# The openings of four feed-forward networks: when weight parts are made ahead of activations, and when side transfers begin

## The chip, the cores and the metric

One Trainium2 chip, one of its cores. The metric is the device time of one execution in microseconds (us). The kernel before takes 2700.04 us, the median of three runs (2699.19 to 2700.79).

A core has TensorE (PE, the matrix engine; its weight load is listed apart as PEld), VectorE (DVE), ScalarE (ACT), GpSimd (POOL) and SyncE (SP). Each takes its instructions in the order in which they are written; semaphores join them. Transfers between HBM and the on-chip memory run on 16 DMA engines. Here SP issues the loads of the weights and POOL issues the side transfers, in two DMA queues (q1 and q0).

## The reference

Two blocks of two layers each, all in float32, 256 tokens of width 1024. The change touches the first block's four plain networks, `swiglu`, numbered 0 to 3 here ("the first" to "the fourth"), and the loading of the second block's modulation weights, which are worked on beside them:

```python
def rms_norm(x, g, eps=NORM_EPS):
    x32 = x.astype(jnp.float32)
    y = x32 * lax.rsqrt(jnp.mean(x32 * x32, axis=-1, keepdims=True) + eps)
    return (y * g.astype(jnp.float32)).astype(x.dtype)

def swiglu(h, w_gate, w_up, w_down):
    return (jax.nn.silu(h @ w_gate) * (h @ w_up)) @ w_down

    for layer in range(DEPTH):
        x = x + 0.5 * swiglu(rms_norm(x, ffn_norm[layer, 0]), ffn_w_gate[layer, 0],
                             ffn_w_up[layer, 0], ffn_w_down[layer, 0])
        h = rms_norm(x, mix_norm[layer])
        ...                       # attention mixer (layer 0) or RWKV-7 time mixing (layer 1)
        x = x + 0.5 * swiglu(rms_norm(x, ffn_norm[layer, 1]), ffn_w_gate[layer, 1],
                             ffn_w_up[layer, 1], ffn_w_down[layer, 1])

def adaln(cond, w_mod, b_mod):    # second block: per layer, for two condition vectors
    m = jax.nn.silu(cond) @ w_mod + b_mod
    return [t[:, None, :] for t in jnp.split(m, N_MOD, axis=-1)]
```

So the order is: network 0, attention, network 1, network 2, RWKV-7, network 3, and then the second block with three more networks of another make, which the change leaves alone.

## The kernel before

**Weights.** All weights are packed in the order of use as tiles of 16 blocks of 128x128 floats, 1 MB each. SP loads them one after the other into a ring of three slots (`ring`); the load of tile T waits until TensorE has begun tile T-2 (semaphore `freed`). TensorE multiplies float32 as three products of rounded parts. Of each tile ScalarE copies the high part (`high(t)`, L1624, two halves) into one of two buffers `w_parts`, VectorE subtracts to get the low part (`low(t)`, L2158, two halves), and TensorE does three matmuls a block (L616, L617, L618). As there are two buffers, `high(t)` waits for the load of tile t and for TensorE having begun tile t-1.

**A network** has 33 tiles. Tiles come in threes: 16 blocks of gate, 16 of up, 16 of down weights, for 256 columns of the hidden width; `gate` and `up` write a PSUM bank each, the activation (silu of one times the other) is made by ScalarE and VectorE, and `down` adds into four banks. Numbered from 0: tile 0 is the first gate, 1 the first up, 2 and 3 are the second gate and up, 4 is the first down, 5 and 6 are the third gate and up, 7 is the second down, and so on.

**The opening.** The first gate and up tiles work on x times the gain (`h_parts`), before the root of the mean square is known. When VectorE has its reciprocal (L2294), the product of gate 0 is scaled (`scale_gate(0)`, L2260), ScalarE takes the silu in place (`scaled_silu(0)`, L1656) and VectorE finishes the activation (`scaled_activation(0)`, L2264, L2184, L2187 and one L2158). Tiles 2 and 3 are still done on `h_parts`, with `scale_gate(1)` and so on after them. From tile 5 on TensorE reads the normed input, `normed_parts`, which VectorE (eight instructions of L2302), ScalarE (`normed_high`, L1651) and VectorE again (`normed_low`) make in the opening. After tile 6 the order is that of a loop (L1686, L2315).

**The closing.** The last down tile ends bank by bank, and VectorE adds each of four banks to x (L2342, `x_ready`; after the mixers L2348). The next network's tile 0 is split before that: ScalarE's `high_first` stands ahead of `scaled_high` (which copies the four quarters of x as `h_parts`, L1645), and VectorE's `first_low(2, (0,))` stands ahead of the first add and `first_low(2, (1,))` ahead of the third. After RWKV-7 both halves of `first_low(3)` stand ahead of all four adds.

**Side transfers.** Beside each of the four networks a quarter of the second block's modulation runs: POOL loads two condition rows, spread over the partitions (0.5 MB each), and eight groups of modulation weights (1.5 MB each) into two buffers, `mod_w[0]` and `mod_w[1]`; VectorE works a group off in each half step of the loop (L2245) and counts `mod_used`, 8 to a network. Groups from the third on wait for their buffer. All of it stands in POOL's `ffn(n)`, L469 to L485. In the fourth network the context and the rope tables (1 MB and 0.6 MB) come first.

## Time and profile before

| | |
|---|---|
| median of three runs | 2700.04 us |
| the profiled execution: its time, its span | 2704.08 us, 2700.3 us |
| TensorE busy, weight load busy | 2652.0 us (98%), 2458.9 us (91%) |
| VectorE, ScalarE, POOL busy | 2121.3 us, 1292.1 us, 109.4 us |
| chain that ended last | PE 88%, DVE 5%, ACT 3%, DMA 3% |
| tile loads | 374 of 1024 KB, 4.8 us from issue to landing (median) |
| modulation weights, condition rows | 32 of 1536 KB, 8.2 us; 8 of 512 KB, 6.6 us |

Busy TensorE is nearly the whole span; what is not its own work is a few stalls, each found in the timeline as a matmul with idle time before it and the engine that ended it. A time in a timeline is counted from the span's start; merged rows have a count, and their length runs from the first's start to the last's end. The profile of one execution is 2704.08 us against a median of 2700.04 us, so differences are worked out inside the profile and then put on the median.

### The profile page before, as it was taken

The page shows a single profiled execution, that of the slowest core. Times are in us where ns is not written, and L with a number is a line of the kernel's source. Part 1 is how long each engine was busy: PE and PEld are TensorE (multiplying, and loading weights), DVE is VectorE, ACT ScalarE, POOL GpSimd, SP SyncE. Part 2 cuts the span into 40 slices and gives each one's busy share as a digit, 9 for nine tenths or more (in the row PEclk, how much of TensorE's full clock was granted, in tenths as well). Part 3 has the DMA queues.
Part 4 walks back from the last instruction along what each step waited for, and adds up shares of the span by engine and source line. Part 5 has one row for each costly group of instructions (what it writes and reads, how often), then busy time and mean ns, then how long its engine had stood idle before and what let it go on. Part 6 is the DMA issues. An engine that isn't in the chain of part 4 may idle for free.

```text
span 2700.3 us, 51095 instructions
## 1 busy us (share of the span) xinstructions
PE 2652.0 (98%) x20514; PEld 2458.9 (91%) x20514; DVE 2121.3 (79%) x3219; ACT 1292.1 (48%) x1780; POOL 109.4 (4%) x109
## 2 busy tenths in 40 slices
PE   8999999999999999999999999999999999999999
PEld 7998799999888989999879999986899999859999
DVE  7986589899765647995987878499878887987877
ACT  5345553443532324335565544555554464564543
POOL 0000000000013310000000000000000000000000
PEclk9999999999999999999999999999999999999999
DMA  7764267667431015764424455431345544404454
GB/s 273 280 233 157 94 258 279 238 253 280 155 140 63 1 73 219 280 233 172 157 79 156 166 185 183 168 141 63 110 156 187 188 156 155 153 19 145 168 186 155
DMA packets 61229, 456.22 MB, mean 169 GB/s; under 512 B 6840, under 2 KB 6864, under 8 KB 8736
## 3 DMA queue, kind: packets, MB, share of 16 engines
q1 hardware_dynamic: 54432, 395.86, 40.1%
q0 software_dynamic: 6656, 58.35, 5.4%
q8 instruction: 104, 1.70, 0.2%
q14 instruction: 37, 0.30, 0.0%
HBM read 453.12 MB, written 1.07 MB: 168 GB/s over the span
## 4 chain that ended last, share of the span: by engine, by line
PE 88%; DVE 5%; ACT 3%; DMA 3%; issue 1%; DVEq 0%; SPq 0%; ACTq 0%
PE ps L777 22%; PE ps L616 14%; PE ps L617 14%; PE ps L618 14%; PE ps L1058 3%; DMA ring<-in_weights 3%; PE ps L1452 3%; PE ps L1459 1%; ACT arena L2087 1%; PE ps L1311 1%; PE ps L1148 1%; PE ps L1141 1%; PE ps L558 1%; PE ps L1294 1%; DVE w_parts L2158 1%
## 5 line engine op out<-in xcount | busy, mean ns | idle before, releaser
L1624 ACT ACTIVATE w_parts<-ring 128x1024 fp32r<-128x1024 f32 x462 | 463.4, 1052 | 402.3 <-PE ps L616 284.9
L616 PE MATMUL ps<-normed_parts,w_parts 128*128 128x256 f32 x2160 | 602.3, 279 | 1.7 <-DVE w_parts L2158 1.7
L617 PE MATMUL ps<-normed_parts,w_parts 128*128 128x256 f32 x2160 | 603.7, 279 | 0.0
L618 PE MATMUL ps<-normed_parts,w_parts 128*128 128x256 f32 x2160 | 603.0, 279 | 0.0
L2158 DVE SCALAR_TENSOR_TENSOR w_parts<-ring,w_parts 128x1024 fp32r<-128x1024 f32 x462 | 544.6, 1220 | 50.0 <-ACT w_parts L1624 49.4
L777 PE MATMUL ps<-stream_high,half_parts 128*128 128x256 f32 x2224 | 422.8, 286 | 2.5 <-DVE half_parts L2363 1.6
L616 PEld LDWEIGHTS ps<-normed_parts,w_parts 128*128 128x128 f32 x2160 | 406.0, 188 | 2.3 <-DVE w_parts L2158 2.3
L618 PEld LDWEIGHTS ps<-normed_parts,w_parts 128*128 128x128 f32 x2160 | 406.0, 188 | 0.0
L617 PEld LDWEIGHTS ps<-normed_parts,w_parts 128*128 128x128 f32 x2160 | 405.9, 188 | 0.0
L2363 DVE SCALAR_TENSOR_TENSOR half_parts<-ring,half_parts 128x1024 fp32r<-128x1024 f32 x225 | 271.9, 1213 | 130.3 <-ACT half_parts L1711 129.4
L777 PEld LDWEIGHTS ps<-stream_high,half_parts 128*128 128x128 f32 x2224 | 347.9, 188 | 7.6 <-issue 5.6
L616 PE MATMUL ps<-act_parts,w_parts 128*128 128x256 f32 x1232 | 344.2, 279 | 1.9 <-DVE w_parts L2158 1.6
L617 PE MATMUL ps<-act_parts,w_parts 128*128 128x256 f32 x1232 | 344.3, 279 | 0.0
L618 PE MATMUL ps<-act_parts,w_parts 128*128 128x256 f32 x1232 | 344.0, 279 | 0.0
L1711 ACT ACTIVATE half_parts<-ring 128x1024 fp32r<-128x1024 f32 x225 | 235.9, 1059 | 204.9 <-PE ps L777 174.3
L777 PE MATMUL ps<-stream_low,half_parts 128*128 128x256 f32 x1112 | 310.4, 279 | 0.0
L616 PEld LDWEIGHTS ps<-act_parts,w_parts 128*128 128x128 f32 x1232 | 231.6, 188 | 3.5 <-DVE w_parts L2158 2.6
L2245 DVE CUSTOM_DVE_ANT_0 arena<-arena 128x1024 f32<-128x1024 f32 x192 | 227.2, 1221 | 7.6 <-DVE vec L2325 6.5
L618 PEld LDWEIGHTS ps<-act_parts,w_parts 128*128 128x128 f32 x1232 | 231.6, 188 | 0.0
L617 PEld LDWEIGHTS ps<-act_parts,w_parts 128*128 128x128 f32 x1232 | 231.5, 188 | 0.0
L777 PEld LDWEIGHTS ps<-stream_low,half_parts 128*128 128x128 f32 x1112 | 209.3, 188 | 3.3 <-issue 3.1
L2824 DVE SCALAR_TENSOR_TENSOR arena<-arena,vec 128x256 f32<-128x256 f32 x360 | 154.1, 480 | 2.3
(459 smaller groups left out, 4197.2 us busy)
## 6 DMA issues: line engine op xcount, KB each, us to landing
ring<-in_weights SPq DMA_DIRECT2D x374, 1024.0 KB, 4.8
arena<-in_mod_weights POOLq DMA_DIRECT2D x32, 1536.0 KB, 8.2
arena<-in_cond POOLq DMA_DIRECT2D x8, 512.0 KB, 6.6
arena<-toeplitz_rows POOLq DMA_DIRECT2D x1, 1536.0 KB, 12.3
x<-in_x SPq DMA_DIRECT2D x1, 1024.0 KB, 4.7
arena<-in_ctx POOLq DMA_DIRECT2D x1, 1024.0 KB, 5.4
out<-x SPq DMA_DIRECT2D x1, 1024.0 KB, 3.9
const<-in_const SPq DMA_DIRECT2D x1, 999.0 KB, 11.4
```

Source lines behind the costliest of these rows:

```text
L616: first = pe.matmul(into, wh, high, start=start, stop=False, skip_group_check=True)
L617: pe.matmul(into, wh, low, start=False, stop=False, skip_group_check=True)
L618: return first, pe.matmul(into, wl, high, start=False, stop=stop, skip_group_check=True)
L777: mm = pe.matmul(into, stationary, moving, start=start and n == 0, stop=stop and n == 2, skip_group_check=True)
L1058: mm = pe.matmul(ps[:, mm_n[0] % 4, m * S:(m + 1) * S], w.take(), mixed[i][:, k, :], start=(k == 0), stop=(k == KT - 1))
L1452: mm = pe.matmul(ps[:, two_banks(j) + tt, 0:keys], q[:, tt * P:(tt + 1) * P], k, start=True, stop=True)
L1624: a(w_parts[:, to, 0, cols], ring[:, at, cols], ACT.Copy).then_inc(s["w_high"], 1)
L1711: a(half_parts[:, u % 3, 0, :], ring[:, tile % RING, half * HALF:(half + 1) * HALF], ACT.Copy).then_inc(s["half_high"], 1)
L2158: return stt(out=out, in0=whole, scalar=1.0, in1=high, op0=ALU.mult, op1=ALU.subtract)
L2245: ins = nc.vector.tensor_tensor_reduce(into, mod_w[half][:, q, :], cond_row[c], 1.0, 0.0, ALU.mult, ALU.add, mod_part[:, at, c:c + 1])
L2363: stt(out=half_parts[:, u % 3, 1, :], in0=ring[:, (t["tile"] + tile) % RING, half * HALF:(half + 1) * HALF], scalar=1.0, in1=half_parts[:, ...
L2824: ins = stt(out=conv[:, b, :], in0=src, scalar=wt, in1=conv[:, b, :], op0=ALU.mult, op1=ALU.add)
```

## The change

Two edits. In the opening, ScalarE does `high(3)` ahead of `scaled_silu(0)`; VectorE does `low(3)` ahead of `scaled_activation(0)`, `low(4)` ahead of the eight instructions that norm the input, and `scale_gate(1)` after `normed_low`. On POOL's queue other waits stand ahead of the side transfers: the second group of network 0 waits for its second gate product; network 1's condition rows and first group wait for the last logits of the attention (`dl_max`) and its second group for the x after it; network 2's wait for the last modulation group of network 1; network 3's wait for nothing of their own.

```diff
@@ -475,11 +475,17 @@
-                if n:
-                    pool.wait_ge(s["x_ready"], (0, 2, 3, 5)[n] * QUARTERS)
+                if n == 1:
+                    pool.wait_ge(s["dl_max"], GROUP)
+                if n == 2:
+                    pool.wait_ge(s["mod_used"], 2 * MOD_ROUNDS)
                 for c in range(2):
                     pool.dma_start(cond_row[c], d["cond"][:, c * D:(c + 1) * D].broadcast_to((P, D))).then_inc(s["cond_in"], 16)
                 for g in range(MOD_ROUNDS):
+                    if n == 0 and g == 1:
+                        pool.wait_ge(s["gate_ready"], 2)
+                    if n == 1 and g == 1:
+                        pool.wait_ge(s["x_ready"], 2 * QUARTERS)
@@ -1673,8 +1679,8 @@
+                high(3)
                 scaled_silu(0)
-                high(3)
                 high(4)
                 normed_high()
                 scaled_silu(1)
@@ -2293,8 +2299,9 @@
                 scale_gate(0)
+                low(3)
                 scaled_activation(0)
-                low(3)
+                low(4)
                 if ahead:
                     dve.wait_ge(s["std_ready"], NORMS[ahead["i"]] + 1)
...
+                normed_low()
                 scale_gate(1)
-                low(4)
-                normed_low()
                 low(5)
                 scaled_activation(1)
                 low(6)
```

In the kernel after, POOL's and ScalarE's lines stand 6 lower in the file, VectorE's 6 or 7, and POOL's DMAs at L483 and L491.

VectorE in the opening of each network, from the scaling of gate 0 to the second activation; the pairs of L2158 rows on `ring` are `low(3)`, `low(4)`, `low(5)` in this order. Before:

```order
L2260 TENSOR_TENSOR arena<-ps,rstd 128x512 [waits gate_ready,dve_step]
L2264 TENSOR_TENSOR arena<-arena,rstd 128x512 [waits gate_used]
L2184 TENSOR_TENSOR arena<-ps,arena 128x512 [waits up_ready,dve_step]
L2187 CAST act_parts<-arena 128x512 [waits dve_step]
L2158 SCALAR_TENSOR_TENSOR act_parts<-arena,act_parts 128x512 [waits dve_step]
L2158 SCALAR_TENSOR_TENSOR w_parts<-ring,w_parts 128x1024 [waits w_high] x2
L2302 SCALAR_TENSOR_TENSOR h<-x,vec,rstd 128x256 x8
L2260 TENSOR_TENSOR arena<-ps,rstd 128x512 [waits gate_ready]
L2158 SCALAR_TENSOR_TENSOR w_parts<-ring,w_parts 128x1024 [waits w_high] x2
L2158 SCALAR_TENSOR_TENSOR normed_parts<-h,normed_parts 128x512 [waits normed_high] x4
L2158 SCALAR_TENSOR_TENSOR w_parts<-ring,w_parts 128x1024 [waits w_high] x2
L2264 TENSOR_TENSOR arena<-arena,rstd 128x512 [waits gate_used]
```

The same place in the kernel after:

```order
L2266 TENSOR_TENSOR arena<-ps,rstd 128x512 [waits gate_ready,dve_step]
L2164 SCALAR_TENSOR_TENSOR w_parts<-ring,w_parts 128x1024 [waits w_high] x2
L2270 TENSOR_TENSOR arena<-arena,rstd 128x512 [waits gate_used]
L2190 TENSOR_TENSOR arena<-ps,arena 128x512 [waits up_ready,dve_step]
L2193 CAST act_parts<-arena 128x512 [waits dve_step]
L2164 SCALAR_TENSOR_TENSOR act_parts<-arena,act_parts 128x512 [waits dve_step]
L2164 SCALAR_TENSOR_TENSOR w_parts<-ring,w_parts 128x1024 [waits w_high] x2
L2309 SCALAR_TENSOR_TENSOR h<-x,vec,rstd 128x256 x8
L2164 SCALAR_TENSOR_TENSOR normed_parts<-h,normed_parts 128x512 [waits normed_high] x4
L2266 TENSOR_TENSOR arena<-ps,rstd 128x512 [waits gate_ready]
L2164 SCALAR_TENSOR_TENSOR w_parts<-ring,w_parts 128x1024 [waits w_high] x2
L2270 TENSOR_TENSOR arena<-arena,rstd 128x512 [waits gate_used]
```

Tile 3's low part now stands ahead of the first activation, tile 4's ahead of the norming, and the scaling of gate 1 (the second row `arena<-ps,rstd`) directly ahead of tile 5's low part.

ScalarE in the same opening, from the root to tile 5; rows `w_parts<-ring` that wait are the first halves of `high(3)`, `high(4)`, `high(5)`. Before:

```order
L1592 ACTIVATE std<-ps 128x256 [waits ss_ready]
L1656 ACT_TABLE_LOAD
L1656 ACTIVATE arena<-arena 128x512 [waits gate_scaled]
L1624 ACTIVATE w_parts<-ring 128x1024 [waits freed,tile_loaded0]
L1624 ACTIVATE w_parts<-ring 128x1024
L1624 ACTIVATE w_parts<-ring 128x1024 [waits freed,tile_loaded1]
L1624 ACTIVATE w_parts<-ring 128x1024
L1651 ACTIVATE normed_parts<-h 128x512 [waits h_ready] x4
L1656 ACTIVATE arena<-arena 128x512 [waits gate_scaled]
L1624 ACTIVATE w_parts<-ring 128x1024 [waits freed,tile_loaded2]
```

The same place in the kernel after:

```order
L1598 ACTIVATE std<-ps 128x256 [waits ss_ready]
L1630 ACTIVATE w_parts<-ring 128x1024 [waits freed,tile_loaded0]
L1630 ACTIVATE w_parts<-ring 128x1024
L1662 ACT_TABLE_LOAD
L1662 ACTIVATE arena<-arena 128x512 [waits gate_scaled]
L1630 ACTIVATE w_parts<-ring 128x1024 [waits freed,tile_loaded1]
L1630 ACTIVATE w_parts<-ring 128x1024
L1657 ACTIVATE normed_parts<-h 128x512 [waits h_ready] x4
L1662 ACTIVATE arena<-arena 128x512 [waits gate_scaled]
L1630 ACTIVATE w_parts<-ring 128x1024 [waits freed,tile_loaded2]
```

Only tile 3's high part moved; the table load for silu now comes after it, and the second silu still stands ahead of tile 5's high part.

POOL's queue around the third and fourth networks; the first four rows are the third network's side transfers, the rest the fourth's (`in_ctx` is the context). Before:

```order
L481 DMA arena<-in_cond 128x1024 [waits x_ready]
L481 DMA arena<-in_cond 128x1024
L485 DMA arena<-in_mod_weights 128x3072 x2
L485 DMA arena<-in_mod_weights 128x3072 [waits mod_used] x6
...
L476 DMA arena<-in_ctx 128x2048 [waits y_ready]
L477 DMA arena<-in_rope 128x1280
L481 DMA arena<-in_cond 128x1024 [waits x_ready]
```

And in the kernel after:

```order
L483 DMA arena<-in_cond 128x1024 [waits mod_used]
L483 DMA arena<-in_cond 128x1024
L491 DMA arena<-in_mod_weights 128x3072 x2
L491 DMA arena<-in_mod_weights 128x3072 [waits mod_used] x6
...
L476 DMA arena<-in_ctx 128x2048 [waits y_ready]
L477 DMA arena<-in_rope 128x1280
L483 DMA arena<-in_cond 128x1024 x2
L491 DMA arena<-in_mod_weights 128x3072 x2
```

The third network's condition rows wait for a count that is reached inside the second network; the fourth's follow the rope tables with no wait between.

## Rows read from the trace of the kernel before

**Rows 1.** Timeline, TensorE: start, us, engine, line, operation, count, [idle before <-releaser].
```profile
33.11 0.36 PE L616 MATMUL ps<-h_parts,w_parts 128*128 128x256 f32 x1 [2.08 <-DVE w_parts L2158]
356.69 0.48 PE L616 MATMUL ps<-h_parts,w_parts 128*128 128x256 f32 x1 [1.92 <-DVE w_parts L2158]
548.53 0.36 PE L616 MATMUL ps<-h_parts,w_parts 128*128 128x256 f32 x1 [2.12 <-DVE w_parts L2158]
1049.20 0.36 PE L616 MATMUL ps<-h_parts,w_parts 128*128 128x256 f32 x1 [2.06 <-DVE w_parts L2158]
```

**Rows 2.** Busy time by stretch: us, PE, PEld, DVE, ACT, POOL, PEclk, DMA, GB/s.
```profile
350.00:355.00 5.00, 4.76 (x41) 4.57 (x40) 4.16 (x6) 3.30 (x4) 0.00 (x0) 1.00 1.01 428
355.00:360.00 5.00, 3.31 (x16) 3.34 (x17) 5.00 (x10) 2.07 (x3) 0.00 (x0) 0.68 0.58 206
```

**Rows 3.** Timeline, ScalarE, third network's opening, 540 to 558.
```profile
541.26 1.28 ACT L1656 ACT_TABLE_LOAD   x1
546.07 2.00 ACT L1624 ACTIVATE w_parts<-ring 128x1024 fp32r<-128x1024 f32 x2 [1.65 <-DMA ring<-in_weights]
554.37 0.62 ACT L1656 ACTIVATE arena<-arena 128x512 f32<-128x512 f32 x1
555.02 2.01 ACT L1624 ACTIVATE w_parts<-ring 128x1024 fp32r<-128x1024 f32 x2
```

**Rows 4.** Timeline, VectorE, openings of the second, third and fourth networks.
```profile
351.41 0.69 DVE L2260 TENSOR_TENSOR arena<-ps,rstd 128x512 f32<-128x512 f32 x1
...
543.06 0.69 DVE L2260 TENSOR_TENSOR arena<-ps,rstd 128x512 f32<-128x512 f32 x1
544.45 0.69 DVE L2264 TENSOR_TENSOR arena<-arena,rstd 128x512 f32<-128x512 f32 x1 [0.70 <-ACT arena L1656]
...
557.89 2.35 DVE L2158 SCALAR_TENSOR_TENSOR w_parts<-ring,w_parts 128x1024 fp32r<-128x1024 f32 x2
...
1042.91 0.69 DVE L2260 TENSOR_TENSOR arena<-ps,rstd 128x512 f32<-128x512 f32 x1
```

**Rows 5.** Timeline, TensorE, tile 5 begins in the same three openings.
```profile
369.61 0.28 PE L616 MATMUL ps<-normed_parts,w_parts 128*128 128x256 f32 x1
...
560.25 0.28 PE L616 MATMUL ps<-normed_parts,w_parts 128*128 128x256 f32 x1
...
1062.04 0.28 PE L616 MATMUL ps<-normed_parts,w_parts 128*128 128x256 f32 x1
```

**Rows 6.** DMA issues at 517.0, 534.6, 343.0 and 1034.5, in this order.
```profile
ring<-in_weights SPq DMA_DIRECT2D x1, 1024.0 KB, 4.7
ring<-in_weights SPq DMA_DIRECT2D x1, 1024.0 KB, 11.4
ring<-in_weights SPq DMA_DIRECT2D x1, 1024.0 KB, 10.2
ring<-in_weights SPq DMA_DIRECT2D x1, 1024.0 KB, 12.2
```

**Rows 7.** Timeline, GpSimd's queue, third and fourth networks.
```profile
529.08 1.05 POOL L481 DMA_DIRECT2D arena<-in_cond  x2 [50.22 <-DVE x L2342]
...
999.64 0.59 POOL L476 DMA_DIRECT2D arena<-in_ctx  x1 [0.94 <-DVE h L2646]
```

**Rows 8.** Timeline, VectorE and ScalarE, from the second network's end to the third's beginning.
```profile
511.52 0.17 DVE L2325 TENSOR_TENSOR vec<-vec,arena 128x12 f32 x1 [0.17 <-DVE arena L2245]
...
523.66 1.23 DVE L2158 SCALAR_TENSOR_TENSOR w_parts<-ring,w_parts 128x1024 fp32r<-128x1024 f32 x1 [2.65 <-ACT w_parts L1624]
...
528.10 0.69 DVE L2342 SCALAR_TENSOR_TENSOR x<-ps,x 128x512 f32<-128x512 f32 x1 [0.28 <-PE ps L618]
...
527.85 1.89 ACT L1645 ACTIVATE h_parts<-x,vec 128x256 fp32r<-128x256 f32 x4 [0.62 <-DVE x L2342]
```

**Rows 9.** Timeline, ScalarE, before the fourth network.
```profile
1019.51 2.01 ACT L1624 ACTIVATE w_parts<-ring 128x1024 fp32r<-128x1024 f32 x2 [22.31 <-DMA ring<-in_weights]
...
1028.68 0.91 ACT L1645 ACTIVATE h_parts<-x,vec 128x256 fp32r<-128x256 f32 x2 [0.82 <-DVE x L2348]
```

## Prediction, written before the kernel after was run

> **What bounds the kernel now.** TensorE is busy nearly throughout, so I first listed its idle times in its timeline and kept those in the plain networks. Each opening has one of 2 us, at the first matmul of tile 3, which waits for VectorE's low part [rows 1]; together 2.08 + 1.92 + 2.12 + 2.06 = 8.2 us. Next came the busy time by stretch, because from tile 3 to tile 5 the second opening takes 369.61 - 356.69 = 12.9 us and the third only 560.25 - 548.53 = 11.7 [rows 1, 5]. In the stretch behind the second's stall the granted clock is 0.68, and 16 matmuls take 3.31 us, 0.207 us each, against 4.76 / 41 = 0.116 at full clock [rows 2]. So the engine ran some 3.3 us at 1.2 of 2.4 GHz after standing still for 1.9 us; that costs 16 x 0.091 = 1.5 us. The fourth opening (1062.04 - 1049.20 = 12.8) has such a spell too, the third has none, and I take none for the first, whose stall is like the third's. What the openings lose is thus 8.2 + 2 x 1.5 = 11.2 us at most.
>
> Why tile 3 is late is seen on ScalarE and VectorE: tile 3's high part begins at 546.07, after 1.65 us of waiting for its load [rows 3], and VectorE's low part stands behind the first activation, which itself waits 0.70 us for silu [rows 4]. The load took 11.4 us from its issue, and 10.2 and 12.2 in the second and fourth openings, where one issued before the side transfers takes 4.7 [rows 6]; POOL has issued its 4 MB 5.5 us before [rows 7]. The DMA engines are then full, at 428 GB/s [rows 2].
>
> **The openings.** The stall at tile 3 goes, in all four. With the side transfers issued earlier, tile 3's load is there in time (in the first network only its first group is ahead, 1.5 MB less, 3.7 us at 428 GB/s). In the third opening ScalarE starts tile 3's high part at 541.3, is done with it at 543.3, loads the table in 1.28 us [rows 3] and has the silu by 545.3; VectorE meanwhile makes the low part from 543.75 to 546.0. TensorE needs it at 546.4 and has it.
>
> What is late next is tile 5. ScalarE works in order: the second silu waits for `scale_gate(1)`, and that now stands behind `normed_low`, so tile 5's high part can't begin sooner. VectorE's work between the scaling of gate 0 and tile 5's low part is the same instructions as before in another order: 557.89 - 544.45 = 13.4 us without idle time [rows 4]. From the scaling's end, 543.06 + 0.69, that gives 557.2; then silu 0.62 and half of tile 5's high part, 2.01 / 2 [rows 3], with 0.1 for the hand-overs: 558.9; then half of the low part, 2.35 / 2 [rows 4]: 560.1. Before, tile 5 began at 560.25 [rows 5]. So the third opening gains 0.15 us: the stall moves from tile 3 to tile 5, where it is 2.1 + 0.15 less, about 1.9 us. The first opening is like it, 0.15. In the second the same 17.0 us from the scaling's start give 351.41 + 17.0 = 368.4 against 369.61, 1.2 us; in the fourth 1042.91 + 17.0 = 1059.9 against 1062.04, 2.1 us [rows 4, 5]. Sum 3.6 us, the two slow spells already gone in it. But four stalls of 1.5 to 2.2 us are there again, and before two of four such brought the slow clock: I put back two spells, 3.1 us. Openings: -3.6 + 3.1 = -0.5 us. Bounds: no spell -3.6, four spells +2.6.
>
> **The third network's side transfers.** They now wait for the count that VectorE completes at 511.4, just ahead of its sum at 511.52 [rows 8], 17.6 us sooner than at 529.08 [rows 7]. That falls into the closing of the second network. The tile load issued 5.5 us after the burst is then no longer tile 3 but tile 0 of the third network, issued at 517.0 [rows 6]. Issued so, three loads took 10.2, 11.4 and 12.2; I take the middle: it lands at 528.4 instead of 521.7. Queued behind it, in order: half its high part on ScalarE 1.05, half the low part on VectorE (1.23), two adds, the other half, two adds (0.6 each), and ScalarE's last quarter of h (0.9), 6.8 us with overlaps of pipeline ends [rows 8]. The last quarter is then ready at 535.2 instead of 527.85 + 1.89 = 529.74: 5.5 us late, and TensorE has little else to do. It stands idle for some 4 us in this, more than before the slow spells, so 1.5 us for one spell: +7.0 us. Bounds: landing after 10.2 us and no spell, +4.3; after 12.2 us and two spells, +9.4. What before hid in the opening (only tile 3) now meets the wait that TensorE can't be given other work for.
>
> **The fourth network's side transfers** wait for nothing of their own and follow the context at 999.64 [rows 7]. The queue then holds 1 + 0.6 + 1 + 3 MB, and SP's two tiles of the output projection come beside them: 8.0 million bytes, at 428 GB/s [rows 2] 18.7 us, until 1020. Tile 0's load is issued at 1014.7, into the last group's transfer. It landed at 1019.4, as ScalarE waited for it until 1019.51 [rows 9]; with half the burst gone I take 10.3 us, 1025.0. VectorE's and ScalarE's row of work behind it is as long as above, 6.8 us: 1031.8 against 1028.68 + 0.91 = 1029.6 [rows 9], +2.2 us. With a slow spell at even chance 0.8: +3.0. Bounds: nothing at all (it lands by 1022.8) and 12.2 us with two spells, 4.1 + 3.1 = +7.2. The projection's own last tile is issued one tile's work earlier and has the work of two to land: I count nothing for it.
>
> **The second network's** rows and first group start when the attention's softmax is nearly done, at a time without tile loads; its second group, alone, is issued when all four were before. Nothing is late by them: 0. **The first network's** second group waits for the second gate product, which ends where tile 3 begins (31 us, the stall's start in [rows 1]), and is first read in the loop; it shares the engines with tile 5's load, which is not wanted before the second silu, 10 us later: 0.
>
> **Sum.** -0.5 + 7.0 + 3.0 = +9.5 us within the profiled execution (2704.08 us, span 2700.3). The runs' median lies 4 us lower than it, with the same work, so I put the difference on the median: 2700.04 + 9.5 = 2709.5 us.
>
> A rule of the Trainium skill that speaks against the 11.4 us: DMA: Bandwidth & Descriptors, section "Queues, rings and completion order", says that each DMA engine goes round-robin between the queues that have work, packet by packet. By that, a tile beside the side transfers would get about half the engines and take some 7 to 9 us. The 10.2 to 12.2 of [rows 6] don't agree with it for a load issued just behind the condition rows.
>
> **Rivals.**
> - *The queues share evenly (same).* The shares would be by packets of 8 and 12 KB, 40% for the tile: its 1.05 MB at 0.4 x 428 GB/s take 6.1 us instead of 2.5, so 4.7 + 3.6 = 8.3 us. Tile 0 lands at 525.3, +2.4 us in the third network, and 1023.0, +0.2, in the fourth. Openings -0.5: +2.1, 2702.1 us. For it: only part of a burst is the rows, the slow beginning. Against: three of three loads so issued took longer.
> - *Tile 0's load goes first, the closings are untouched (faster).* Then only openings remain, -3.6 without spells: 2696.4 us. Against it the same three rows.
> - *Tile 5 is not late.* Then the openings give all of 11.2 us and the closings take 10: -1.2, 2698.8 us. It would need ScalarE to do tile 5's high part ahead of the second silu, which the order denies.
> - *All new gaps slow the clock (slower still).* Two more spells in the openings, one more in each closing: +9.5 + 3.1 + 1.5 + 0.8 = +14.9, 2714.9 us. The gaps in the closings are the longest.
>
> **How the numbers follow.** Forecast 2709.5 us with 0.60; even sharing 0.15; closings untouched 0.09; tile 5 not late 0.04; all spells 0.12. A measurement of this kernel tells 0.2%, 5.4 us, from no change. Slower by over that: nearly all of the first case, all of the last: 0.71. Faster by over that asks for untouched closings and a gain of the openings beyond 3.6 us, or both the second and third rival at once: 0.06. Same: 0.23. The range leaves out the untouched closings and half of the third rival at its lower end and little at its upper: 2700 to 2716 us.
>
> **What the profile after would show.** Right: no idle time at tile 3 and one of 1.5 to 2.2 us at tile 5 in each opening, released by VectorE; a tile load issued near 516 that takes over 10 us; ScalarE waiting for DMA ahead of the third network's tile 0 for some 6 us; the adds to x there 5 us later. Wrong: the tile load near 516 under 7 us, or TensorE reaching the third network's tile 1 no later than 534 less what the first two openings gain. If the closings cost nothing the whole forecast falls to the openings' half microsecond.

## The result and the profile after

The kernel after takes 2717.71 us (median of 9 runs, 2714.52 to 2719.61), against 2700.79 us for the kernel before in runs beside it. The ratio is 1.0056, 95% interval 1.0043 to 1.0069, so the change costs 11.6 to 18.6 us. The profiled execution took 2714.52 us with a span of 2712.6, against 2704.08 and 2700.3. The two spans differ by 12.3 us, and that is what the traces account for. The ratio and the medians give 15 to 17 us. The two profiled executions lie on opposite sides of their medians (before 3.3 us over, after 3.2 us under), and the other executions left no trace, so these 3 to 5 us stay unexplained.

The stalls of the plain networks are in TensorE's timeline of the kernel after, with the columns of [rows 1]. The L668 rows are the first matmuls of a network, the L622 rows tile 5:

```profile
45.92 0.35 PE L622 MATMUL ps<-normed_parts,w_parts 128*128 128x256 f32 x1 [3.15 <-DVE w_parts L2164]
...
371.95 0.55 PE L622 MATMUL ps<-normed_parts,w_parts 128*128 128x256 f32 x1 [2.38 <-DVE w_parts L2164]
...
535.00 0.47 PE L668 MATMUL ps<-h_parts,w_parts 128*128 128x256 f32 x2 [3.99 <-ACT h_parts L1651]
...
537.25 0.79 PE L668 MATMUL ps<-h_parts,w_parts 128*128 128x256 f32 x2 [0.74 <-ACT h_parts L1651]
...
570.53 0.35 PE L622 MATMUL ps<-normed_parts,w_parts 128*128 128x256 f32 x1 [2.39 <-DVE w_parts L2164]
...
1040.86 0.47 PE L668 MATMUL ps<-h_parts,w_parts 128*128 128x256 f32 x2 [1.86 <-ACT h_parts L1651]
...
1073.57 0.36 PE L622 MATMUL ps<-normed_parts,w_parts 128*128 128x256 f32 x1 [1.67 <-DVE w_parts L2164]
```

The four stalls of [rows 1] at tile 3 are gone. In each opening there is one at tile 5 in their place, 9.6 us together against 8.2, and two networks now begin with a stall that waits for ScalarE's parts of h. What delays these is seen on GpSimd's queue, ScalarE and VectorE; the rows to compare are [rows 7], [rows 8] and [rows 9]:

```profile
514.81 1.05 POOL L483 DMA_DIRECT2D arena<-in_cond  x2 [32.54 <-DVE arena L2251]
515.85 1.05 POOL L491 DMA_DIRECT2D arena<-in_mod_weights  x2
...
531.00 2.00 ACT L1630 ACTIVATE w_parts<-ring 128x1024 fp32r<-128x1024 f32 x2 [8.96 <-DMA ring<-in_weights]
532.09 1.23 DVE L2164 SCALAR_TENSOR_TENSOR w_parts<-ring,w_parts 128x1024 fp32r<-128x1024 f32 x1 [8.01 <-ACT w_parts L1630]
...
1035.73 1.06 ACT L1630 ACTIVATE w_parts<-ring 128x1024 fp32r<-128x1024 f32 x1 [27.45 <-DMA ring<-in_weights]
```

The burst (the condition rows and two groups of weights, 4 MB) begins at 514.81; in the kernel before it began at 529.08. Tile 0's load of the third network is issued at 520.11 and lands at 530.92, that of the fourth is issued at 1025.79. From issue to landing (last column, us) they take 10.8 and 9.8, where the kernel before took 4.7 for the third network's [rows 6]:

```profile
ring<-in_weights SPq DMA_DIRECT2D x1, 1024.0 KB, 10.8
...
ring<-in_weights SPq DMA_DIRECT2D x1, 1024.0 KB, 9.8
```

Busy time by stretch behind the third network's late start, columns as in [rows 2]:

```profile
530.00:535.00 5.00, 1.01 (x9) 0.84 (x8) 2.91 (x4) 3.05 (x5) 0.00 (x0) 1.00 0.80 338
535.00:540.00 5.00, 4.02 (x17) 3.53 (x18) 5.00 (x11) 4.37 (x11) 0.00 (x0) 0.54 0.62 210
540.00:545.00 5.00, 5.00 (x36) 5.00 (x36) 3.93 (x6) 1.96 (x3) 0.00 (x0) 0.78 0.01 3
```

TensorE does 1.01 us of work in 5, and in the next two stretches of 5 us its granted clock is 0.54 and 0.78 in the mean: it ran at 1.2 of 2.4 GHz from about 535.4 to 542.2, twice as long as the spell of [rows 2].

**Where the time went.** Both kernels, and those below, issue the same 20,514 matmuls in the same order, so each one's start can be set against its start before. By how much that difference grows in a part of the program is what the part costs; a closing is counted up to the next network's tile 1. The names of the other kernels are explained with their experiments. In us against the kernel before, one profiled execution each:

| | start, to 28 | 1st opening | 2nd opening | 3rd closing | 3rd opening | 4th closing | 4th opening | elsewhere | span |
|---|---|---|---|---|---|---|---|---|---|
| after | +0.5 | +2.4 | 0.0 | +7.4 | -0.2 | +2.5 | -1.5 | +1.2 | +12.3 |
| order only | -0.5 | +5.6 | +4.9 | +0.2 | +5.4 | 0.0 | +4.2 | +3.6 | +23.6 |
| waits only | -0.2 | -0.2 | +0.3 | +6.5 | +0.9 | +4.2 | -2.1 | -1.0 | +8.6 |
| late transfers | -0.1 | +3.1 | -1.0 | -0.1 | +5.2 | 0.0 | +3.1 | +0.3 | +10.6 |
| half burst | +0.8 | +0.6 | +1.0 | +4.5 | -0.2 | 0.0 | -1.5 | +2.0 | +7.1 |
| rows last | +0.7 | -0.1 | +0.5 | +6.4 | -0.2 | +2.0 | -1.6 | +1.7 | +9.4 |
| tile 5 ahead | -0.4 | +1.2 | -3.6 | +5.9 | -2.5 | +4.1 | -3.3 | -2.1 | -0.4 |
| spread | +0.7 | +0.4 | -0.9 | 0.0 | +1.4 | 0.0 | -1.6 | -2.5 | -2.3 |
| spread, tile 5 ahead | +0.4 | -2.3 | -2.5 | 0.0 | -2.4 | 0.0 | -3.3 | +3.6 | -6.6 |
| late, tile 5 ahead | +0.3 | -1.5 | -3.6 | -0.1 | +2.1 | 0.0 | 0.0 | -0.5 | -3.1 |
| spread, order as before | -0.6 | -0.2 | +1.5 | +0.6 | -0.2 | 0.0 | -2.1 | -2.2 | -3.1 |

The 3rd closing is the second network's end up to the third's tile 1, the 4th the output projection up to the fourth's tile 1; both are named by the network whose tile 0 may be late. The second opening's column holds that network's beginning too. By rounding and at the ends a row's sum differs from its span by up to 0.3. Each profiled execution lies somewhere in its kernel's spread (that of before 3 us over the median beside it, that of order only 5 over, that of spread 5 under). So the medians and their intervals below decide whether a kernel is faster, and the table tells only where the time goes.

### The profile page after: what moved, and what is told of

The parts are those of the page before. It is cut to its first block, busy times and chain, and to the rows that moved or that the text cites. A ratio compares the mean times of both kernels' runs of the same rounds, so it can differ in the third digit from the quotient of the medians.

```text
span 2712.6 us, 51095 instructions
## 1 busy us (share of the span) xinstructions
PE 2658.1 (98%) x20514; PEld 2464.3 (91%) x20514; DVE 2120.3 (78%) x3219; ACT 1291.5 (48%) x1780; POOL 109.5 (4%) x109
## 4 chain that ended last, share of the span: by engine, by line
PE 86%; DVE 7%; ACT 3%; DMA 2%; issue 1%; DVEq 0%; SPq 0%; ACTq 0%
PE ps L783 21%; PE ps L622 14%; PE ps L623 14%; PE ps L624 14%; PE ps L1064 3%; PE ps L1458 3%; DMA ring<-in_weights 2%; DVE w_parts L2164 1%; PE ps L1465 1%; ACT arena L2093 1%; PE ps L1317 1%; PE ps L1154 1%; PE ps L1147 1%; PE ps L564 1%; PE ps L557 1%
## 5 line engine op out<-in xcount | busy, mean ns | idle before, releaser
L622 PE MATMUL ps<-normed_parts,w_parts 128*128 128x256 f32 x2160 | 604.3, 280 | 11.3 <-DVE w_parts L2164 11.3
L622 PEld LDWEIGHTS ps<-normed_parts,w_parts 128*128 128x128 f32 x2160 | 407.4, 189 | 12.6 <-issue 10.3
L622 PE MATMUL ps<-act_parts,w_parts 128*128 128x256 f32 x1232 | 344.5, 280 | 1.3 <-DVE w_parts L2164 1.2
L622 PEld LDWEIGHTS ps<-act_parts,w_parts 128*128 128x128 f32 x1232 | 231.5, 188 | 2.7 <-DVE w_parts L2164 1.9
```

Source lines behind the costliest of these rows:

```text
L622: first = pe.matmul(into, wh, high, start=start, stop=False, skip_group_check=True)
```

## The experiments

Theory A is that of the forecast: early side transfers make tile 0's load late where TensorE has nothing else to do, and the new order moves the openings' stall from tile 3 to tile 5. Its rivals were that the loss comes from one of the two alone, that the order gains and the transfers cost, or that the two are one effect. The letters of the rivals begin anew in each expectation. The names are those of the table.

The runs of before beside each kernel gave 2702.41, 2701.72 and 2700.98 us (medians of 11, 33 and 19 runs). Line numbers in the rows differ by two to six between kernels.

**Order only**: the new order of the openings, the waits of before. That is the kernel after with GpSimd's side of the change undone; against the kernel after the edit is:

```
-                if n == 1: pool.wait_ge(s["dl_max"], GROUP)
-                if n == 2: pool.wait_ge(s["mod_used"], 2 * MOD_ROUNDS)
+                if n: pool.wait_ge(s["x_ready"], (0, 2, 3, 5)[n] * QUARTERS)
-                    if n == 0 and g == 1: pool.wait_ge(s["gate_ready"], 2)
-                    if n == 1 and g == 1: pool.wait_ge(s["x_ready"], 2 * QUARTERS)
```

> Only the new order of the openings; the side transfers start as in the kernel before. Theory A (the closings cost the time, the new order needs the early transfers): no cost in the closings; but tile 3's load is late again (10 to 12 us), and silu of gate 0 now stands behind tile 3's high part on ScalarE. Tile 5 begins 14.0 us after the first activation does, which begins some 4 us after tile 3's load lands: 48.6, 371.2, 564.0 and 1064.7 us against 44.8, 369.6, 560.3 and 1062.0, +11.9 us, and 0 to 6 us of slow clock behind stalls of some 5 us at tile 5. Total +12 to +18 us. Rival B (the order is worth its 2 us a stall by itself): -4 to -8 us. Rival C (the order is neutral, as worked out with early transfers): -0.5 us.

Measured: 2721.99 us, ratio 1.0071 (1.0058 to 1.0084), which is 16 to 23 us slower than before; theory A had 12 to 18. TensorE's stalls in the second and fourth openings:

```profile
361.46 0.36 PE L616 MATMUL ps<-h_parts,w_parts 128*128 128x256 f32 x1 [1.36 <-DVE w_parts L2158]
377.04 0.55 PE L616 MATMUL ps<-normed_parts,w_parts 128*128 128x256 f32 x1 [4.14 <-DVE w_parts L2158]
...
1066.39 0.36 PE L616 MATMUL ps<-h_parts,w_parts 128*128 128x256 f32 x1 [1.88 <-DVE w_parts L2158]
1081.97 0.36 PE L616 MATMUL ps<-normed_parts,w_parts 128*128 128x256 f32 x1 [4.14 <-DVE w_parts L2158]
```

The closings cost at most 0.2 us, and the openings cost 20 us. With late transfers tile 3's load is late as before, so its stall stays, and the one at tile 5 comes on top, at 2.60 to 4.14 us, where the expectation had some 5. The order alone is a loss. In the traces it is larger than that of the whole change (23.6 against 12.3 us); the intervals of the two ratios overlap.

**Waits only**: the new waits, the openings' order of before. Against the kernel before it is the edit above read the other way round.

> Only the new waits of the side transfers; the openings are in the old order. Theory A: the closings cost as in the changed kernel, 7.7 us before the third network and 3.2 before the fourth; tile 3's load is in time but its low part still stands behind the first activation, so the stall at tile 3 stays at 1.9 us in each opening (each 0.2 us shorter). Total +9 to +12 us. Rival B (the cost of the change is the slow clock behind the new gaps at tile 5): -1 to +1 us. Rival D (the queues share evenly): +2 us.

Measured: 2710.96 us, ratio 1.0037 (1.0023 to 1.0051), 10 us where theory A had 9 to 12.

```profile
32.93 0.36 PE L622 MATMUL ps<-h_parts,w_parts 128*128 128x256 f32 x1 [1.92 <-DVE w_parts L2164]
357.66 0.36 PE L622 MATMUL ps<-h_parts,w_parts 128*128 128x256 f32 x1 [1.92 <-DVE w_parts L2164]
530.70 1.50 PE L668 MATMUL ps<-h_parts,w_parts 128*128 128x256 f32 x4 [3.29 <-ACT h_parts L1651]
...
554.36 0.41 PE L622 MATMUL ps<-h_parts,w_parts 128*128 128x256 f32 x1 [1.92 <-DVE w_parts L2164]
```

The closings cost 6.5 and 4.2 us without any change of order. Tile 3's stall stays at 1.92 us in three openings, and is 1.05 us in the fourth, although its load is in time now: it had two causes, the load and VectorE's order, and either is enough.

**Late transfers**: the kernel after, the third and fourth networks' wait put back.

```
-                if n == 2: pool.wait_ge(s["mod_used"], 2 * MOD_ROUNDS)
+                if n >= 2: pool.wait_ge(s["x_ready"], (0, 2, 3, 5)[n] * QUARTERS)
```

> The changed kernel with the waits of the third and fourth networks' side transfers put back (x ready). Theory A: TensorE has no gap above 0.5 us before these networks; but their tile 3 is late again with silu behind it, tile 5 begins 22.7 us after the reciprocal's start in the third and 23.6 in the fourth (18.8 with early transfers). First and second networks as in the changed kernel. Total +4 to +9 us, so less than the change by 6 to 12. Rival B (the cost is in all four openings alike): the whole +15 stays. Rival C (only the closings matter, the openings are even): -0.5 us.

Measured: 2712.77 us, ratio 1.0042 (1.0028 to 1.0057), which is 11.3 us (8 to 15) where theory A had 4 to 9. Both closings are at zero, as expected. The expectation also had tile 5 begin 3.9 and 4.8 us later in the two openings than with early transfers; against the kernel after they cost 5.4 and 4.6 us more, as much as the closings gain. The third's rows on ScalarE and TensorE:

```profile
546.78 2.00 ACT L1630 ACTIVATE w_parts<-ring 128x1024 fp32r<-128x1024 f32 x2 [4.49 <-DMA ring<-in_weights]
...
549.24 0.36 PE L622 MATMUL ps<-h_parts,w_parts 128*128 128x256 f32 x1 [1.78 <-DVE w_parts L2164]
...
564.82 0.40 PE L622 MATMUL ps<-normed_parts,w_parts 128*128 128x256 f32 x1 [4.14 <-DVE w_parts L2164]
```

**Half burst**: the kernel after, the third and fourth networks' second group of weights behind the last residual sum.

```
-                    if n == 1 and g == 1: pool.wait_ge(s["x_ready"], 2 * QUARTERS)
+                    if n >= 1 and g == 1: pool.wait_ge(s["x_ready"], (0, 2, 3, 5)[n] * QUARTERS)
```

> The changed kernel, but the second group of modulation weights (1.5 MB) of the third and fourth network waits for the last residual sum: the early burst is 2.5 MB instead of 4. Theory A (what delays tile 0's load is the bytes still ahead of it when it is issued, 5.3 us behind the burst's start): the third network's load lands in 6 to 8 us instead of 10.8, its closing costs 1 to 3 us instead of 7.4, the fourth's 0 to 1 instead of 2.5; the openings as changed: +4 to +8. Rival B (any transfer of the other queue under way halves the load's rate, however many bytes are behind): the load takes 9 to 11 us all the same, +10 to +13. Rival C (the condition rows, with their broadcast to 128 partitions, are what blocks the queue, not the weights): the same, +10 to +13, and the load's landing follows the rows'.

Measured: 2708.38 us, ratio 1.002 (1.0011 to 1.0029), 5.4 us where theory A had 4 to 8. The third network's load takes 8.5 us from issue to landing:

```profile
ring<-in_weights SPq DMA_DIRECT2D x1, 1024.0 KB, 8.5
```

and the third network starts with a stall of 1.73 us (3.99 in the kernel after) and a second one of 1.03 (0.74), in TensorE's timeline:

```profile
533.38 0.47 PE L668 MATMUL ps<-h_parts,w_parts 128*128 128x256 f32 x2 [1.73 <-ACT h_parts L1651]
```

The 8.5 us lie between theories A (6 to 8) and B (9 to 11). The third closing costs 4.5 us in place of 7.4, more than A's 1 to 3, and the fourth nothing in place of 2.5.

**Rows last**: the kernel after, but the condition rows behind both groups.

```
-                for c in range(2): pool.dma_start(cond_row[c], ...)
+                for c in range(2 if n < 2 else 0): pool.dma_start(cond_row[c], ...)
                 for g in range(MOD_ROUNDS):
                     ...
+                    if n >= 2 and g == 1:
+                        for c in range(2): pool.dma_start(cond_row[c], ...)
```

> The changed kernel, but in the third and fourth network the two groups of modulation weights are issued ahead of the condition rows; the same 4 MB. Theory A (the tile load is held back twice: its first packets come 3.4 us behind its issue while the rows' 4 KB packets are under way, and from there on it alternates with 12 KB packets and has 40% of the rate): with groups ahead its first packets come 1.3 to 2 us behind the issue, it lands in 7.5 to 8.5 us instead of 10.8, the third closing costs 3 to 5 us instead of 7.4: +5 to +10 in all. Rival B (the burst's bytes ahead of it hold it back, whatever they are): 10 to 11 us, +11 to +14 as the changed kernel. Rival C (groups ahead are worse, their packets being three times as long): over 11 us, +15 or more.

Measured: 2711.08 us, ratio 1.0035 (1.0022 to 1.0047), 9.4 us (6 to 13); the third network's load takes 9.6 us, where theory A had 7.5 to 8.5 and B 10 to 11, and the third closing costs 6.4 us where A had 3 to 5. Theory A's share of the queues was right, its cause of the late beginning wrong. The DMA queues by stretch (packets, MB, share of the 16 engines; q0 GpSimd's, q1 SP's), first the kernel after from 520.11 to 523.4, then from 524 to 529:

```profile
q0 software_dynamic: 240, 1.33, 101.9%
...
q0 software_dynamic: 114, 1.20, 56.5%
q1 hardware_dynamic: 114, 0.93, 44.0%
```

and rows last from 522 to 525:

```profile
q0 software_dynamic: 63, 0.77, 60.4%
q1 hardware_dynamic: 61, 0.50, 39.6%
```

For 3.3 us behind its issue not one packet of the load runs; then the queues take turns, 114 packets to 114 (16 of GpSimd's are of under 512 B, the others of 12 KB) and 61 to 63 with rows last. A load with the engines free has its first packet 0.96 to 0.99 us behind the issue (three loads from 517.05 on in the kernel before); behind a burst it is 3.45 us in the kernel after and 3.44 with rows last, where weights stand ahead. So the late beginning does not come from the rows. The rest of the 9.6 us is an estimate: an engine has 8 packets of 8 KB of the load, each with one of 12 KB, 0.31 + 0.46 us by the packets' mean durations, 6.2 us, and 3.4 + 6.2 = 9.6 us. Why the kernel after needs 1.2 more stays open. The rows' own packets are not the reason: the rows had landed at 522.74, and the load's first packet ran at 523.56.

What does shorten the late beginning is less data ahead. With the rows alone issued 5.3 us ahead, 1 MB, as in the kernel "spread, tile 5 ahead" below, the load's first packet runs 1.35 us behind its issue; with 2.5 MB (half burst) it is 3.63 us, no sooner than with 4.

**Tile 5 ahead**: the kernel after, with tile 5's parts before the second part of the activation.

```
                 # ScalarE
                 normed_high()
+                high(5)
                 scaled_silu(1)
-                high(5)
                 ...
                 # VectorE
                 normed_low()
+                low(5, halves=(0,))
                 scale_gate(1)
-                low(5)
+                low(5, halves=(1,))
```

> The changed kernel with tile 5's high part ahead of the second part of the activation and half of its low part ahead of the last scaling. Theory A (the second half of the openings' loss is that the new order leaves tile 5's parts behind the activation, 1.7 to 3.2 us of stall and a stretch at half clock each): all four stalls ahead of tile 5 go, the openings get 4.5, 4.0, 2.6 and 0.5 us shorter, the closings of the second and third network keep their +7 and +2.5: +12 - 11.6, within 2 us of the kernel before. Rival B (the work of the activation only moves, and tile 6 or the next stage waits instead): the stalls ahead of tile 5 come back elsewhere, +9 to +12, as the changed kernel. Rival C (the stretches at half clock come whatever the stalls are): only the stalls' own 10 us minus what is hidden, +4 to +7.

Measured: 2702.35 us, ratio 1.0006 (0.9997 to 1.0015): by the ratios 13.5 us less than the kernel after, and within 2 us of before as theory A had it. What remains of stalls:

```profile
43.96 0.36 PE L622 MATMUL ps<-normed_parts,w_parts 128*128 128x256 f32 x1 [1.82 <-DVE w_parts L2164]
...
528.29 0.47 PE L668 MATMUL ps<-h_parts,w_parts 128*128 128x256 f32 x2 [3.33 <-ACT h_parts L1651]
...
1030.33 0.47 PE L668 MATMUL ps<-h_parts,w_parts 128*128 128x256 f32 x2 [1.95 <-ACT h_parts L1651]
```

Three of four stalls at tile 5 are gone and nothing took their place; in the first opening 1.82 of 3.15 us stay, and it gets 1.2 us shorter where 4.5 were expected. The closings cost 5.9 and 4.1 us (7.4 and 2.5 in the kernel after).

**Spread**: the kernel after; in the third and fourth networks the rows early, the first group behind the issue of tile 0's load, the second behind the last residual sum.

```
-                if n == 2: pool.wait_ge(s["mod_used"], 2 * MOD_ROUNDS)
+                    if n >= 2 and g == 0: pool.wait_ge(s["freed"], ffn_tiles[n] - 1)
-                    if n == 1 and g == 1: pool.wait_ge(s["x_ready"], 2 * QUARTERS)
+                    if n >= 1 and g == 1: pool.wait_ge(s["x_ready"], (0, 2, 3, 5)[n] * QUARTERS)
```

> The changed kernel with the side transfers of the third and fourth network spread (rows early, first group behind the issue of tile 0's load, second group behind the last residual sum), tile 5's parts left behind the activation. Theory A (closings and openings add up, and tile 5's stall is its own cost of the new order): the closings cost nothing, the four stalls at tile 5 stay at 1.7 to 3.2 us, which was worth 12 to 15 us between the changed kernel with and without the edit on tile 5: 2 to 8 us slower than before. Rival B (once the loads are in time, the stall at tile 5 goes too): as with the edit, -7 to -10. Rival C (tile 5's stall only takes the place of tile 3's): -2 to +1.

Measured: 2705.13 us, ratio 1.0012 (1.0002 to 1.0022), so 3 us slower (1 to 6) where theory A had 2 to 8. The profiled execution is the shortest of twelve (2699.87), its span 2.3 us under that of before, so its row of the table looks better than its median. The closings are at zero. All four stalls at tile 5 are there:

```profile
46.00 0.36 PE L624 MATMUL ps<-normed_parts,w_parts 128*128 128x256 f32 x1 [2.89 <-DVE w_parts L2166]
...
369.38 0.36 PE L624 MATMUL ps<-normed_parts,w_parts 128*128 128x256 f32 x1 [2.37 <-DVE w_parts L2166]
...
559.37 0.36 PE L624 MATMUL ps<-normed_parts,w_parts 128*128 128x256 f32 x1 [2.37 <-DVE w_parts L2166]
...
1061.45 0.36 PE L624 MATMUL ps<-normed_parts,w_parts 128*128 128x256 f32 x1 [1.66 <-DVE w_parts L2166]
```

**Spread and tile 5 ahead**: both edits.

> The changed kernel with two changes more: side transfers of the third and fourth networks are spread (condition rows as early, first group of modulation weights when TensorE begins the last tile before the network, second group when x is ready), and in the openings tile 5's high part stands ahead of the second silu, half of its low part ahead of the scaling of gate 1. Theory A: no load of a tile 0 takes over 7 us, tile 3 is in time, tile 5 begins 16.5 us after the reciprocal's start against 19.0, 20.0, 19.0 and 20.9 before: -10 to -13 us. If tile 5's gap is not due to ScalarE's order it stays, 1.5 to 2.4 us in each opening, and the kernel is 0 to 4 us faster. If early side transfers harm the closings however spread, it is +5 us or more.

Measured: 2693.61 us, ratio 0.9967 (0.9955 to 0.998): 9 us (5 to 12) faster than the kernel before, and the only one that beats it. Theory A had a gain of 10 to 13. In the plain networks' openings and closings TensorE has no stall over 0.6 us, and the granted clock is full:

```profile
40.00:45.00 5.00, 4.83 (x42) 4.65 (x41) 5.00 (x7) 3.39 (x5) 0.00 (x0) 1.00 0.53 202
...
530.00:535.00 5.00, 5.00 (x44) 5.00 (x43) 4.30 (x6) 2.92 (x3) 0.00 (x0) 1.00 0.83 307
```

The third network's tile 0 takes 5.6 us from issue to landing. Theory A's 10 to 13 us are all there up to 1080 (10.8 us ahead of before); from there to 1500 it gives 4.6 back, 3.4 of them in the fourth network by 1160, where TensorE stands idle for 1.68, 1.04 and 1.40 us (at 1097.94, 1116.06 and 1134.53); the kernel before has one such stall there, 0.93 us. In the same stretch ScalarE waits longer for tile loads than before, first 6.06 us against 5.31. That the loads beside the side transfers set this pace is likely, and not tested.

**Late and tile 5 ahead**: late transfers with tile 5's parts ahead.

> The changed kernel with the side transfers of the third and fourth network back behind the last residual sum, and tile 5's parts ahead of the second part of the activation. Theory A (late transfers cost nothing in the closings but keep tile 3's load of the next opening late, since it is issued behind them): closings +0, a stall of 1.8 to 2.1 us ahead of tile 3 in the third and fourth opening as in the kernel before, none ahead of tile 5: 2 to 5 us faster than before, so slower than the staggered transfers by 4 to 7. Rival B (the stall ahead of tile 3 goes once the order is changed): as the staggered ones, -8 to -10. Rival C (tile 5's parts cost as much elsewhere): +5 to +10, as the same kernel without the edit on tile 5.

Measured: 2701.08 us, ratio 0.9997 (0.9988 to 1.0006), so from 3 us faster to 2 slower.

```profile
543.05 0.36 PE L622 MATMUL ps<-h_parts,w_parts 128*128 128x256 f32 x1 [2.18 <-DVE w_parts L2164]
556.31 0.36 PE L622 MATMUL ps<-normed_parts,w_parts 128*128 128x256 f32 x1 [1.81 <-DVE w_parts L2164]
...
1045.38 0.36 PE L622 MATMUL ps<-h_parts,w_parts 128*128 128x256 f32 x1 [0.62 <-DVE w_parts L2164]
```

The stall at tile 3 is back in the third opening as A had it, but only 0.62 us in the fourth, and there is one at tile 5 of 1.8 us in both, which A had denied. The gain of 2 to 5 us that A had is not seen.

**Spread, order as before**: the spread waits with the order of before.

> The kernel before, in its own order of the openings, with the side transfers of the third and fourth network spread: rows early, first group behind the issue of tile 0's load, second group behind the last residual sum. Theory A: closings within 1 us of before; the stall ahead of tile 3 stays near 1.9 us in the first and second opening, 1 to 1.9 in the others, since VectorE's order sets it: -1 to -4 us. Rival B (the spread alone brings all that the spread with both edits of order brought): -7 to -10. Rival C (early rows hurt the closings by themselves): +2 to +5.

Measured: 2701.99 us, ratio 1.0005 (0.9996 to 1.0014), so from 1 us faster to 4 slower, where theory A had a gain of 1 to 4. The closings are within 0.6 us, and the stalls at tile 3 are those of waits only (1.92, 1.92, 1.92, 1.05). Loads in time bring no gain that these runs can tell while VectorE's order makes tile 3 late.

## Why the prediction was right, step by step

- **The number.** The forecast was 2709.5 us in a range of 2700 to 2716. The ratio puts the change at +15 us, so at 2715.2 us on the forecast's base of 2700.04; that is just inside the range, and the median as measured, 2717.71, is just above it. The size was thus forecast too low, by 2.8 us in the traces (+12.3 for +9.5) and by 6 to 7 by the ratio and the medians. The rival "all new gaps slow the clock" had 2714.9 us, the nearest number, but its mechanism is not what the trace shows: it has four spells of slow clock in all openings, two in the third closing and one in the fourth, and the profiled execution has two, two (one of double length) and none. The forecast had two, one and an even chance.
- **The stall at tile 3 goes.** Right: none left.
- **It comes back at tile 5.** Right in place and releaser. Only one of the four stalls is within the 1.5 to 2.2 us that were named as the sign (1.67); the others are 2.38, 2.39 and 3.15. The table has -0.2 us for the third opening and -1.5 for the fourth, near the working. The first is the miss: I took it to be like the third, 0.15 us gained, and it costs 2.4. ScalarE there waits 1.46 us for tile 3's load, and the silu that now stands behind tile 3 starts at 31.18 instead of 28.39; the stall of 3.15 us was followed by a slow spell (granted clock 0.66 from 47 to 52). The sum of the four openings was -0.5 us in the forecast and is +0.7 in the trace. ScalarE's timeline of the kernel after and the stretch:

```profile
27.86 2.01 ACT L1630 ACTIVATE w_parts<-ring 128x1024 fp32r<-128x1024 f32 x2 [1.46 <-DMA ring<-in_weights]
```

```profile
47.00:52.00 5.00, 5.00 (x32) 5.00 (x32) 4.90 (x7) 2.25 (x3) 0.00 (x0) 0.66 0.59 211
```

- **The third closing, +7.0.** It is +7.4, the largest term, with its mechanism: the load lands 10.8 us behind its issue, VectorE's low part begins at 532.09 against 523.66 [rows 8], 3.0 us of which were lost before, and TensorE stands idle for 3.99 us and then works at half clock. Of the signs, the adds to x behind it come 5.4 us later once those 3.0 are taken off, for 5 forecast, and ScalarE waits 8.96 us for the load, for some 6. Half burst takes the closing's cost to 4.5, late transfers and spread to zero.
- **The fourth closing, +3.0.** It is +2.5 in the kernel after and 4.2 in waits only, where a slow spell (1039.2 to 1042.6) came with it; the half chance that I gave one was the right doubt. Half burst takes this closing to zero, so the last group of weights is what delays that load. The forecast had it landed by 1020 (its 18.7 us from 999.64 give 1018.3); it landed at 1035.46 in the kernel after, which is 24.7 us behind the context's issue.
- **The second network and the first's second group at 0.** Right for the second opening as a sum (0.0); the second network's beginning has a stall of 0.4 to 0.9 us in some of the kernels, too small to settle.
- **What queues are.** My 11.4 us for the load were taken from like cases and not from a mechanism; that the load then took 10.8 shows the cases were alike, not that I knew why. The rival of even shares (8.3 us for the load) had the packets right and lacked the late beginning. The Trainium skill's rule (DMA: Bandwidth & Descriptors, "Queues, rings and completion order") is that an engine goes round-robin between queues packet by packet. The trace agrees once the load has begun, with 114 packets to 114; whether the profile's packets, here one row of 8 or 12 KB each, are the packets that the page means, no run shows. The late beginning, 3.45 us for 0.96 with free engines, in which the other queue has all the engines, does not follow from it.
- **Left over.** From +9.5 to +12.3 us in the traces: 1.2 us in the openings, -0.1 in the two closings together, 0.5 in the start and 1.2 elsewhere, a spell of slow clock at 931 among them. The 3 to 5 us more of the ratio and the medians have no known cause. More spells in the executions without a trace don't fit: the profiled one has a mean granted clock of 0.996 and is the shortest of the nine, and the eight others, up to 5.1 us longer, have 0.995 to 0.998.

The two halves of the change don't add up: order only costs 19 us, waits only 10, both 15. The new order needs tile 3's load in time, and so the transfers early. Issued early in one burst, they delay the load that the closing hangs on. And the order leaves tile 5's parts behind the second silu and the scaling ahead of it, wherever the transfers are. Spreading the transfers removes the late load, and making tile 5's parts first removes its stall; of the kernels run, only the one with both gains.

## What to carry to other kernels

When large side transfers are moved to an earlier place, look which load is issued within some 5 us behind them, and what waits for it. A late load costs what the order behind it leaves uncovered. In the openings' old order it cost at most 2 us, as much of tile 3's stall was there without it (2.12 us with the late load and 1.92 without in the third, 2.06 and 1.05 in the fourth). In the new order it cost some 5 us there (late transfers against the kernel after), and in the third closing 7. Issue such transfers in pieces, the large ones behind that load. When parts of a tile are moved ahead of other work, follow the tile after next on the same engine, since its parts are what the moved work now stands in front of.

## What the runs showed of the hardware

- A tile load's first packet runs 0.96 to 0.99 us behind its issue on free DMA engines. When the other queue's burst of 2.5 or 4 MB was issued 5.0 to 5.6 us earlier, it runs 3.35 to 3.63 us behind, whatever packets (4 or 12 KB) that burst begins with. With only 1 MB of rows issued 5.3 us earlier it is 1.35 us (spread, tile 5 ahead), and with a single group of 1.5 MB about 2.1 (2.20 for the load at 588.70 in the kernel before).
- Once the load has begun, the two queues have as many packets each, so the share by bytes goes with the packets' lengths: 0.50 of 1.27 MB for 8 KB against 12 KB packets (rows last), 39.6% of the engines' time.
- The condition rows, 4 KB packets, were landed 6.6 and 7.9 us behind the burst's start in the kernel after, with 3 MB behind them.
- A stall of one length was sometimes followed by a stretch at half clock and sometimes not: at tile 3 in the kernel before 1.92 and 2.06 us were, 2.08 and 2.12 weren't; in the kernel after at tile 5 3.15 and 2.38 were, 2.39 and 1.67 weren't. In no profiled execution did the openings or closings have such a stretch without a stall of over 1 us just before or within it.
